# The last gate tile's products spread over five iterations of the unit loop, first half ahead of second, in a decoder-layer kernel

## The reference, cut to what matters

```
h = x @ w_in + b_in                      # ..., z = the last 1024 columns
oa = banded attention (8 query heads, 2 key heads, window 128, sinks)
ob = dilated attention (4 heads, three window/stride pairs)
oc = attention to 256 memory tokens (4 heads)
y = concat(rms(oa), rms(ob), rms(oc)) * g_branch * silu(z)
out = layer_norm(2**0.25 * x + y @ w_out)
```

## Time and profile before

| | us |
|---|---|
| median of 3 runs | 519.87 |
| lowest and highest of them | 519.07, 520.0 |
| span of the profiled execution, first to last instruction | 512.1 |

### The profile page before, as it was taken

One profiled execution on the slowest core, in us unless ns is written; L12 is line 12 of the kernel. 1 busy time (PEld: TensorE's weight loads), 2 busy tenths in 40 slices (PEclk: granted clock), 3 DMA queues, 4 the chain that ended last, 5 costly groups with the idle time before them and its releaser, 6 DMA issues.

```text
span 512.1 us, 9694 instructions
## 1 busy us (share of the span) xinstructions
PE 487.5 (95%) x3480; PEld 443.9 (87%) x3480; DVE 328.4 (64%) x908; ACT 214.9 (42%) x488; POOL 72.7 (14%) x53
## 2 busy tenths in 40 slices
PE   4999999999999979999999898999989999999993
PEld 4999999999999968888888787898878788888882
DVE  4776645557666723444444568878797969798734
ACT  5632222021212035555463659655444454444530
POOL 0000000000000000111101101023232323231425
PEclk9999999999999989999999999999999999999998
DMA  8955472647622453321322179324232414241022
GB/s 288 375 194 146 126 236 82 206 140 257 217 89 93 142 147 105 102 86 56 107 85 91 54 234 316 99 63 135 71 127 60 149 53 148 63 142 48 1 83 82
DMA packets 51710, 67.83 MB, mean 132 GB/s; under 512 B 9552, under 2 KB 41296, under 8 KB 51664
## 3 DMA queue, kind: packets, MB, share of 16 engines
q1 hardware_dynamic: 51088, 66.17, 40.4%
q10 hardware_dynamic: 576, 1.05, 0.6%
HBM read 51.18 MB, written 16.02 MB: 131 GB/s over the span
## 4 chain that ended last, share of the span: by engine, by line
PE 88%; DVE 7%; ACT 2%; DMA 1%; issue 1%; POOLq 0%; POOL 0%; SPq 0%; ACTq 0%; DVEq 0%
PE long_ps L948 15%; PE o_ps L907 9%; PE wide L770 8%; PE wide L772 7%; PE wide L771 7%; PE long_ps L849 5%; PE long_ps L847 5%; PE long_ps L848 5%; PE narrow L887 4%; PE wide L875 4%; PE wide L876 3%; PE wide L781 2%; PE wide L782 2%; PE wide L783 2%; PE narrow L925 1%; DVE nb L1349 1%
## 5 line engine op out<-in xcount | busy, mean ns | idle before, releaser
L770 PE MATMUL wide<-x_hi,w_hi 128*128 128x256 f32 x320 | 88.5, 277 | 0.2
L771 PE MATMUL wide<-x_lo,w_hi 128*128 128x256 f32 x320 | 88.3, 276 | 0.0
L772 PE MATMUL wide<-x_hi,w_lo 128*128 128x256 f32 x320 | 88.3, 276 | 0.0
L770 PEld LDWEIGHTS wide<-x_hi,w_hi 128*128 128x128 f32 x320 | 60.1, 188 | 0.5 <-issue 0.5
L771 PEld LDWEIGHTS wide<-x_lo,w_hi 128*128 128x128 f32 x320 | 60.1, 188 | 0.0
L772 PEld LDWEIGHTS wide<-x_hi,w_lo 128*128 128x128 f32 x320 | 60.1, 188 | 0.0
L1029 ACT ACTIVATE spill<-turn 128x512 fp32r<-128x512 f32 x21 | 13.3, 633 | 99.3 <-DVE turn L1261 73.2
L948 PE MATMUL long_ps<-wo_hi,y_hi 128*128 128x512 f32 x128 | 53.1, 415 | 0.0
L1510 POOL TENSOR_TENSOR g_lo<-g_raw,g_hi 128x1024 fp32r<-128x1024 f32 x6 | 14.3, 2385 | 273.1 <-ACT g_hi L1034 273.1
L948 PE MATMUL long_ps<-wo_lo,y_hi 128*128 128x512 f32 x128 | 52.3, 408 | 0.0
L948 PE MATMUL long_ps<-wo_hi,y_lo 128*128 128x512 f32 x128 | 51.7, 404 | 0.0
(11 more groups left out here) (154 smaller groups left out, 1208.9 us busy)
## 6 DMA issues: line engine op xcount, KB each, us to landing
q_spill<-spill SPq DMA_DIRECT2D x32, 256.0 KB, 2.5
q_pair<-q_spill SPq DMA_DIRECT2D x128, 64.0 KB, 2.0
w_raw<-in_w_qkv SPq DMA_DIRECT2D x12, 512.0 KB, 5.7
x_raw<-in_x_t SPq DMA_DIRECT2D x16, 256.0 KB, 7.7
g_raw<-in_w_gate SPq DMA_DIRECT2D x8, 512.0 KB, 3.5
q_pair<-q_spill SPq DMA_DIRECT2D x32, 128.0 KB, 2.7
q_pair<-q_spill SPq DMA_DIRECT2D x128, 32.0 KB, 1.8
wo_raw<-in_w_out SPq DMA_DIRECT2D x8, 512.0 KB, 4.7
```

The lines of the kernel that those rows point to most:

```text
L770: pe.matmul(dst, w_hi[s][:, k, f], t_hi[:, k, cols], start=(k == 0), stop=False)
L771: pe.matmul(dst, w_hi[s][:, k, f], t_lo[:, k, cols], start=False, stop=False)
L772: mm = pe.matmul(dst, w_lo[s][:, k, f], t_hi[:, k, cols], start=False, stop=(k == KT - 1))
```

## The change

The products of the last tile are listed by part of an iteration in `LAST_TILE`, as pairs (half, k), three matmuls each. There are ten parts, iterations 28 to 32: four pairs in iteration 28, three in each of the others. The first half's k = 7 stands in part 0 of iteration 31, the second's in part 1 of iteration 32. In iteration 28 the second half begins after three k steps of the first instead of after one. `x_used` is told by the second half's product alone. `WO_LOAD_AT` becomes 28, 29, 29, 30, 31, 32, 32, 32 (it was 28, 28, 29, 29, 30, 30, 31, 31), and the four loads behind the last one go to iteration 32. `WO_AT`, counted from 28, becomes 2, 3, 3, 4, 5, 6, 7, 8 (it was 1, 2, 2, 3, 3, 4, 6, 8). The number of matmuls, loads and ACT and DVE instructions is the same.

```diff
-WO_AT = [LAST_TILE_AT + at for at in (1, 2, 2, 3, 3, 4, 6, 8)]
+WO_AT = [LAST_TILE_AT + at for at in (2, 3, 3, 4, 5, 6, 7, 8)]
+LAST_TILE = [((0, 0), (0, 1)), ((0, 2), (1, 0)), ((1, 1), (0, 3)), ((1, 2),), ((0, 4), (1, 3)), ((0, 5),),
+             ((0, 6), (0, 7)), ((1, 4),), ((1, 5), (1, 6)), ((1, 7),)]
...
-WO_LOAD_AT = [LAST_TILE_AT + k // 2 for k in range(FT)]
+WO_LOAD_AT = [LAST_TILE_AT + part // 2 for k in range(FT) for part, made in enumerate(LAST_TILE) if (1, k) in made]
...
-            def last_gate_products(k):
+            def last_gate_products(part):
 
                 f = FT - 1
-                if k == 0:
+                if part == 0:
                     pe.wait_ge(gate_rounded, f + 1)
                     wait_gate_split(f)
-                for h in range(2):
+                for h, k in LAST_TILE[part]:
                     if k == 0:
                         pe.wait_ge(gate_done, 2 * f + h - 1)
...
                     if k == KT - 1:
                         mm.then_inc(gate_full, 1)
-                if k < KT - 1:
-                    mm.then_inc(x_used, 1)
+                    elif h:
+                        mm.then_inc(x_used, 1)
...
-                if f == FT - 1:
-                    last_gate_products(shares * h + share)
+                if v >= LAST_TILE_AT:
+                    last_gate_products(2 * (v - LAST_TILE_AT) + part)
                     return
...
-                if v < GATE_ITERATIONS * GATES:
+                if v < LAST_TILE_AT + len(LAST_TILE) // 2:
                     gate_products(v, part)
```

## The result

The changed kernel ran at 515.13 us at the median of 4 executions (511.96 to 515.92), the kernel before at 519.93 of 4 (519.07 to 521.63). The ratio of the two is 0.9896, its 95% interval 0.9862 to 0.993: faster, by 4.8 us where 3.0 were predicted, and 0.57 us under the predicted range. Measured again beside each other, 12 executions against 35, it was 515.08 against 519.07, ratio 0.9933, interval 0.9907 to 0.9959: 3.5 us by the ratio, 4.0 by the medians.

What follows compares the result with a forecast made beforehand. PE was taken as the bound, with 88% of the last chain, so time is won only where it pauses. 1.66 + 1.7 - 0.3 = 3.06, say 3.0 us, off 519.87 gives 516.9 us; range 515.7 to 518.7.

Steps and rivals of the forecast that it cites:

- the three pauses: PE's waits in iterations 28, 32 and 33, of 1.39, 0.41 and 1.06 us idle, which the change would remove.
- ACT's waits for the loads: ACT's 7.4 us of waiting for first loads would disappear, counted as nothing since no PE instruction was behind them.
- the term for iterations 32 and 33: PE's pauses there would go, worth 1.7 us, between 1.47 by idle time and 1.88 by weight loads.
- the spread of the runs: Some 0.5 us allowed for it at the low end of the predicted range.
- Iteration 28: The second half's first product would no longer wait for DVE's read of half 13; 1.66 us gained.
- The new wait on ACT in 34: PE's transposes wait for unit 32's exponentials; covered by 0.2 to 0.4 us, cost zero, at most 0.3.
- DVE's scaling in 35 to 37: Standing behind `wo_lo`, it would make PE's transposes of outputs wait 0.3 us in sum.
- The sum for the stretch: Gain of 1.66 for iteration 28 plus 1.7 for 32 and 33, less 0.3 for DVE's scaling: 3.06 us.
- a DVE bound: Rival: DVE bounds iterations 33 to 36, 4.8 us lost against 3.36 gained, so slower, 521.3 us; chance 0.07.
- pauses that return elsewhere: Rival: time won in 28 is waited for at the next slower engine; gain under 1.04 us; chance 0.13.
- The first rival: DVE's scaling waits in 35 to 37 total 0.7 to 2 us, leaving a gain of 1.2 to 2.4; chance 0.17.
- the distance between span and time: The runs' median taken as 7.8 us above the profiled span of 512.1 us, and carried over.

Runs made afterwards that it cites:

- e3: The changed kernel with iteration 28's products in the old order, the spread over the later iterations kept; 517.73 us.
- e10: The changed kernel with DVE's scaling of attention outputs ahead of `wo_lo` in an iteration; 514.95 us, ratio 0.9932 to the kernel before.
- e9: The kernel before with GpSimd's layer norm steps cut into pieces of 256 columns; 515.47 us, ratio 0.9945 to the kernel before.
- e1: The kernel before, unedited, timed against itself; 519.0 us, ratio 0.9987.
- e12: The changed kernel with GpSimd's layer norm in pieces, DVE's scaling ahead of `wo_lo` and the four loads in iteration 34; 511.28 us, ratio 0.9859 to the kernel before.
- e2: The changed kernel, unedited, timed again beside the kernel before; 515.08 us, ratio 0.9933.
- e6: The kernel before with only the new `WO_AT` iterations for the output weights, products and loads in the old order; 518.73 us, ratio 0.9976.
- e5: The changed kernel with the old `WO_AT` iterations for the output weights; 527.13 us, ratio 1.0154 to the kernel before.

## Why the prediction was wrong, and what in it was right

The direction was right, and so was the mechanism of the three pauses. The measured time fell out of the range at its low end. The step that failed is the one that put ACT's waits for the loads at nothing, by which the term for iterations 32 and 33 came out too small; the spread of the runs was put too small as well.

**Right, by its steps.** Iteration 28: predicted 1.66 us, measured 1.64 (6.11 to 4.47), more than PE's idle time of 1.39; e3 gives it back alone (1.5). The pauses of 32 and 33: predicted 1.7; iterations 29 to 33 take 18.35 us against 20.27 in the profile that I read, 1.92. The new wait on ACT in 34 had at most 0.3 us to pay. The cover of 0.2 to 0.4 us wasn't there, and 34 takes 3.39 instead of 3.20, as PE's weight loads show in the profile after:

```profile
319.62 0.20 PEld L889 LDWEIGHTS narrow<-ident,prob 128*128 128x128 f32 x2 [0.41 <-ACT prob L1093]
```

DVE's scaling in 35 to 37 was predicted 0.3 late in sum: those three iterations take 11.24 us instead of 10.91, 0.33 lost, and e10 takes that back. With 34 it is 0.52. The sum for the stretch was 3.06 and is 1.64 + 1.92 - 0.52 = 3.04. That it comes so near is in part luck, since the 1.92 hold for the profile that I read and not for the next one. The rivals of a DVE bound and of pauses that return elsewhere didn't come. The first rival's gain was worked out wrong: 3.36 less 0.7 to 2 is 1.4 to 2.7, not 1.2 to 2.4; nothing hangs on it.

**Wrong: ACT's waits for the loads counted as nothing.** The prediction said that no PE instruction was behind them. One was: the wait for tile 4 in iteration 31 stands ahead of the sigmoid, and the sigmoid ahead of the exponentials that PE awaits in 33. In the profile that I read it was 0.78 us; in e9 1.10, in e1 1.53, and 28 to 38 took 41.29 us there. The changed kernel has 0.8 us of waits for these loads left, in two places, with no pause of PE behind them. Against e1 the change is worth 3.84 us, against e9's 40.86 3.4. So the term for 32 and 33, predicted at 1.7, was mis-sized: it measured 1.9 against the profile that I read, where the load came early, and 2.7 against e1. That covers up to 0.8 us of the 1.8 by which the first measurement, 4.8, lies above the 3.0.

**Wrong: the distance between span and time.** I took 7.8 us for what lies around the span and carried it over. It is 1.9 or 2.0 (515.92 - 514.0, and 519.76 - 517.8 in e1). The profile of before was of an execution of some 514 us, 6 us below the median of its runs, and should have been read as a sign that executions of this kernel differ by that much. It doesn't enter the difference, but it hid the next point.

**Wrong: 0.5 us for the spread of the runs.** The kernel before spreads over 514.45 to 521.13 us in the 75 executions timed beside e1 to e12. The profiles show four things that differ between executions: the spacing in the projections (3.9 us up to iteration 1, in one profile of fourteen), the clock in iteration 2 (up to 1.4 us), iteration 50 (2.2 us) and the load of tile 4 (0.8). How much of the spread each one makes isn't shown, since few executions were profiled. The first measurement had three or four executions a side. With 12 against 35 the gain was 3.5 us by the ratio, with 2.1 to 4.8 as its interval. With that interval the range should have reached down to about 519.07 - 4.8 = 514.3. The 0.2% that I took for what can be told from no change was too small as well.

What stays open: whether the 4.8 us of the first measurement hold a part of the change that these profiles miss. The likeliest is chance. Of the profiles without the pieces and with block 1's norm where it was, two of ten escaped the hold in iteration 50 (e2 and e6), too few to say whether the change raises the chance of it.

## What to carry to other kernels

An iteration of a software pipeline without filler is no rest: PE runs ahead in it and then waits for whichever engine got its release late; spread the filler until the last such iteration is covered, and let the half whose successor waits be finished first. When the products that free a buffer are moved, the instructions that wait for its refill must move with them (e5 lost 12 us against the changed kernel, about 2.7 of them to the clock that fell behind its longest pause). Before sizing a change of a few microseconds from one profile, compare that profile's span with the spread of the runs, and read the gain from the stretch between two points of the program.

## What the hardware showed that I had not expected

- A DVE instruction of 128x2 that normally takes 0.16 us took 2.38, as long as a GpSimd instruction of 128x1024 beside it. Cut into four pieces, GpSimd's work grew from 2.37 to 2.98 us and the kernel became 3.5 us faster.
- In a stretch with no idle time of PE and the granted clock at 1.00, one execution issued a 256-column matmul every 113.0 ns and thirteen others every 117.4. The spacing stayed the same for 95 us. What sets it was not tried.
- After a pause of 3.2 to 3.3 us in iteration 2 the granted clock fell for a while in twelve of fourteen executions and not at all in two, with up to 1.5 us of difference between executions of the same code. After the pause of 4.33 us in e5 it fell too; after those of 1.31 us there and 1.63 us in e1 it stayed at 1.00.
